# One block sum of a split down projection, made by VectorE instead of by DMA

## The reference, cut to what matters

```python
def rms_norm(x, g):
    xf = x.astype(jnp.float32)
    y = xf * lax.rsqrt(jnp.mean(xf * xf, axis=-1, keepdims=True) + RMS_EPS)
    return (y * g.astype(jnp.float32)).astype(x.dtype)

def swiglu(h, w_gate, w_up, w_down):
    return (jax.nn.silu(h @ w_gate) * (h @ w_up)) @ w_down

h = rms_norm(x, g_ffn1_pre[l])
x = x + 0.5 * rms_norm(swiglu(h, w_ffn1_gate[l], w_ffn1_up[l], w_ffn1_down[l]), g_ffn1_post[l])
...                                   # stick-breaking attention and retention, merged, projected, added to x
h = rms_norm(x, g_ffn2_pre[l])
x = x + 0.5 * rms_norm(swiglu(h, w_ffn2_gate[l], w_ffn2_up[l], w_ffn2_down[l]), g_ffn2_post[l])
```

## Time and profile before

| | value |
| --- | --- |
| median of three runs | 1460.89 us |
| profiled execution, its own time | 1462.79 us |
| its span, first to last instruction | 1460.9 us |
| busy in the span | PE 95%, PEld 85%, DVE 70%, ACT 53%, POOL 9% |
| mean granted TensorE clock | 0.979 of full speed |
| first down stage, unit 0 to 55 start | 346.42 to 522.54 us |
| second down stage, unit 0 to 55 start | 1276.26 to 1449.15 us |
| plain DMAs, page part 3 | 158.35 MB on SP's and ACT's queues, 34.0% of 16 engines' span |
| accumulating DMAs, page part 3 | 33.56 MB on POOL's queue, 12.5% |

### The profile page before, as it was taken

The page is one execution under the profiler, slowest core; times in us unless marked ns, Lnnn a source line. Parts: engine busy times, 40 slices in busy tenths (PEclk is TensorE's granted clock), DMA queues, the critical chain, the costliest instruction groups (busy, mean ns, idle before and its releaser), DMA issues.

```text
span 1460.9 us, 22674 instructions
## 1 busy us (share of the span) xinstructions
PE 1385.0 (95%) x8648; PEld 1236.7 (85%) x8648; DVE 1019.0 (70%) x1084; ACT 770.1 (53%) x1029; POOL 133.4 (9%) x180
## 2 busy tenths in 40 slices
PE   6999999998798989999989999989999999959997
PEld 6999999997686878767768888789999999948876
DVE  6877788775795954656664343687777887649786
ACT  6554555444676743647763323554445544457763
POOL 0000000001322000332320000000000000023300
PEclk9999999999899999999999999999999999989999
DMA  5323333326999563221112354233233332299974
GB/s 194 102 90 97 115 115 105 97 85 203 285 218 242 178 211 100 74 58 58 44 44 83 90 155 165 86 114 102 85 102 115 115 102 94 94 314 224 254 182 130
DMA packets 161639, 194.48 MB, mean 133 GB/s; under 512 B 6064, under 2 KB 116912, under 8 KB 161456
## 3 DMA queue, kind: packets, MB, share of 16 engines
q1 hardware_dynamic: 143456, 158.35, 34.0%
q0 software_dynamic: 17408, 33.56, 12.5%
q10 hardware_dynamic: 720, 1.84, 0.4%
HBM read 187.43 MB, written 6.29 MB: 133 GB/s over the span
## 4 chain that ended last, share of the span: by engine, by line
PE 81%; DMA 8%; DVE 6%; ACT 3%; issue 1%; POOL 1%; SPq 1%; ACTq 0%; DVEq 0%; POOLq 0%
PE ps L675 14%; PE ps L677 14%; PE ps L678 14%; PE ps L641 5%; PE ps L775 5%; PE ps L777 5%; PE ps L776 5%; PE ps L643 5%; PE ps L642 5%; DMA d_sum<-w_ffn_down 4%; DMA w_raw<-w_ffn_down 3%; PE ps L950 1%; PE ps L648 1%; PE ps L650 1%; PE ps L649 1%
## 5 line engine op out<-in xcount | busy, mean ns | idle before, releaser
L675 PE MATMUL ps<-s_hi,w_hi 128*128 128x256 f32 x960 | 273.2, 285 | 4.8 <-DVE w_lo L1554 4.8
L677 PE MATMUL ps<-s_lo,w_hi 128*128 128x256 f32 x960 | 272.9, 284 | 0.0
L678 PE MATMUL ps<-s_hi,w_lo 128*128 128x256 f32 x960 | 272.9, 284 | 0.0
L675 PE MATMUL ps<-a_hi,w_hi 128*128 128x256 f32 x816 | 232.7, 285 | 3.2 <-DVE a_lo L1509 3.0
L678 PE MATMUL ps<-a_hi,w_lo 128*128 128x256 f32 x816 | 232.4, 285 | 0.0
L677 PE MATMUL ps<-a_lo,w_hi 128*128 128x256 f32 x816 | 232.4, 285 | 0.0
L1127 ACT ACTIVATE w_hi<-w_sum 128x1024 fp32r<-128x1024 f32 x120 | 123.9, 1056 | 175.5 <-DVE w_sum L1581 80.4
L775 PE MATMUL ps<-w_hi,l_hi 128*128 128x512 f32 x448 | 179.2, 400 | 37.0 <-DVE w_lo L1718 37.0
L675 PEld LDWEIGHTS ps<-s_hi,w_hi 128*128 128x128 f32 x960 | 185.6, 193 | 5.1 <-DVE w_lo L1554 5.1
L677 PEld LDWEIGHTS ps<-s_lo,w_hi 128*128 128x128 f32 x960 | 185.7, 193 | 0.0
L678 PEld LDWEIGHTS ps<-s_hi,w_lo 128*128 128x128 f32 x960 | 185.6, 193 | 0.0
(11 more groups left out here) (192 smaller groups left out, 2582.1 us busy)
## 6 DMA issues: line engine op xcount, KB each, us to landing
w_raw<-w_ffn_gate SPq DMA_DIRECT2D x64, 512.0 KB, 4.6
w_raw<-w_ffn_up SPq DMA_DIRECT2D x64, 512.0 KB, 4.9
d_sum<-w_ffn_down POOLq DMA_DIRECT2D x64, 512.0 KB, 12.8
w_raw<-w_ffn_down SPq DMA_DIRECT2D x48, 512.0 KB, 4.9
w_raw<-w_in SPq DMA_DIRECT2D x44, 512.0 KB, 3.9
d_sum<-w_ffn_down SPq DMA_DIRECT2D x32, 512.0 KB, 11.3
x_mid<-x_tok SPq DMA_DIRECT2D x8, 512.0 KB, 4.9
x_tok<-x_mid SPq DMA_DIRECT2D x8, 512.0 KB, 11.0
```

What stands on the lines that cost most here:

```text
L675: pe.matmul(o, wh, hi[:, k, :], start=first and f == 0 and k == 0, stop=False, skip_group_check=True)
L677: pe.matmul(o, wh, lo[:, k, :], start=False, stop=False, skip_group_check=True)
L678: mm = pe.matmul(o, wl, hi[:, k, :], start=False, stop=last and k == KH - 1, skip_group_check=True)
```

## The change

The order of SP's queue changes, and T1 is made in another way. SP loads `d_sum`'s units 0 to 3 with B12 once product 2 of the last pair is over, and units 4 to 7 once product 5 is; ACT negates four units each in turns 0 and 1 instead of two each in turns 0 to 3. For T1 both B12's and B11's unit q come into the raw ring (slots 0 and 1 for even q, 2 and 3 for odd q), and DVE writes their difference to `d_sum` (`sum_t1_down`), two units a turn in turns 14 to 17. Gone with it in each FFN are the eight loads of B11 into `d_sum`, eight negations and eight accumulating DMAs. The loads of `x_tok` go behind those of T1 and the gains, and the fourth round of `down_sum` from turns 12 to 15 to turns 20 to 23.

```diff
-            - (PRODUCTS - 3) * DOWN_UNITS // SLOTS * ((u >= U_V) + (u >= U_END)))
+            - (PRODUCTS - 5) * DOWN_UNITS // SLOTS * ((u >= U_V) + (u >= U_END)))
...
                 sp_eng.wait_ge(t_done, (fi + 1) * N_T)
-                for slot in (RAW11, RAW21, RAW12):
-                    fetch(slot, down_block((0, 0), slot))
+                fetch(RAW11, down_block((0, 0), RAW11))
+                fetch(RAW21, down_block((0, 0), RAW21))
+                sp_eng.wait_ge(unit_done, ud - PRODUCTS + PE_ORDER.index(2) + 1)
+                for q in range(4):
+                    sum_load((0, 1), q)
+                fetch(RAW12, down_block((0, 0), RAW12))
                 fetch(RAW22, down_block((0, 0), RAW22), (w_lo_done, ud))
-
-                sp_eng.wait_ge(unit_done, ud)
-                for q in range(DOWN_UNITS):
+                sp_eng.wait_ge(unit_done, ud - PRODUCTS + PE_ORDER.index(5) + 1)
+                for q in range(4, DOWN_UNITS):
                     sum_load((0, 1), q)
                 for q in range(SLOTS, DOWN_UNITS):
                     fetch(q % SLOTS, down_block((0, 0), q), (w_lo_done, ud + q - SLOTS + 1))
 
-                if fi:
-                    sp_eng.wait_ge(x_left[0], 32)
-                    sp_eng.wait_ge(x_left[1], 32)
-                for t in range(TT):
-                    sp_eng.dma_start(x_tok[:, t, :], x_src[tok(t), :]).then_inc(x_back, 16)
+                for q in range(DOWN_UNITS):
+                    used = (w_lo_done, ud + SLOTS + 2 * q + 2) if q < 2 else (t1_made, DOWN_UNITS * fi + q - 1)
+                    fetch(2 * (q % 2), down_block((0, 1), q), used)
+                    fetch(2 * (q % 2) + 1, down_block((0, 0), q))
 
                 for q in range(SLOTS):
-                    fetch(q, down_block((1, 0), q), (w_lo_done, ud + SLOTS + q + 1))
-
-                for q in range(DOWN_UNITS):
-                    sp_eng.wait_ge(w_lo_done, ud + DOWN_ORDER.index(4) * DOWN_UNITS + q + 1)
-                    sum_load((0, 0), q)
+                    fetch(q, down_block((1, 0), q), (t1_made, DOWN_UNITS * fi + 7 + q // 2))
...                                    # the gains stay here; x_tok's four loads come behind them
-                    for first, begin in ((0, 0), (8, 9), (16, 14)):
-                        if begin <= n < begin + CHUNKS:
-                            for q in (2 * (n - begin), 2 * (n - begin) + 1):
-                                negate(fi, ud, first, q)
+                    if n < 2:
+                        for q in range(4 * n, 4 * n + 4):
+                            negate(fi, ud, 0, q)
+                    if 9 <= n < 9 + CHUNKS:
+                        for q in (2 * (n - 9), 2 * (n - 9) + 1):
+                            negate(fi, ud, 8, q)
...
-                    act_eng.wait_ge(r_full[q], 64 * fi + 16 * ph)
+                    if m == 5:
+                        act_eng.wait_ge(t1_made, DOWN_UNITS * fi + q + 1)
+                    else:
+                        act_eng.wait_ge(r_full[q], 48 * fi + 16 * ph)
...
-                    if n < 4 * CHUNKS:
+                    if n < 3 * CHUNKS:
                         down_sum(fi, n)
+                    elif 5 * CHUNKS <= n < 6 * CHUNKS:
+                        down_sum(fi, n - 2 * CHUNKS)
+                    if 14 <= n < 14 + CHUNKS:
+                        sum_t1_down(fi, ud, 2 * (n - 14))
+                        sum_t1_down(fi, ud, 2 * (n - 14) + 1)
...
+            def sum_t1_down(fi, ud, q):
+
+                turn = raw_turn(ud) + 2 + q // 2
+                slot = 2 * (q % 2)
+                dve.wait_ge(raw_full[slot], turn * 16 + 16)
+                dve.wait_ge(raw_full[slot + 1], turn * 16 + 16)
+                dve.wait_ge(w_lo_done, ud + DOWN_ORDER.index(4) * DOWN_UNITS + q + 1)
+                dve.tensor_tensor(d_sum[:, q, :], w_raw[:, slot, :], w_raw[:, slot + 1, :], ALU.subtract
+                                  ).then_inc(t1_made, 1)
...
-                for step, (j, d) in enumerate(((1, 1), (0, 0), (1, 0), (0, 1))):
+                for step, (j, d) in enumerate(((1, 1), (0, 0), (1, 0))):
```

More of the change, by code:

```diff
@@ L355, in build @@
         r_full = [sem(f"r_full{q}") for q in range(DOWN_UNITS)]
+        t1_made = sem("t1_made")
         r_neg, d_copied, d_summed, y_half, y_whole = (
@@ L563, in ffn_loads @@
                     gain(G_POST2)
+                sp_eng.wait_ge(unit_done, ud)
+                if fi:
+                    sp_eng.wait_ge(x_left[0], 32)
+                    sp_eng.wait_ge(x_left[1], 32)
+                for t in range(TT):
+                    sp_eng.dma_start(x_tok[:, t, :], x_src[tok(t), :]).then_inc(x_back, 16)
                 u = ud + DOWN_ORDER.index(2) * DOWN_UNITS
@@ L1255, in unit_hi @@
                 if m in (1, 2, 3):
-                    turn = raw_turn(ud) + {1: 0, 2: 2, 3: 4}[m] + q // SLOTS
+                    turn = raw_turn(ud) + {1: 0, 2: 6, 3: 8}[m] + q // SLOTS
                     act_eng.wait_ge(raw_full[q % SLOTS], turn * 16 + 16)
@@ L1267, in negate @@
                 else:
-                    act_eng.wait_ge(r_load[q], 32 * fi + (16 if first == 0 else 32))
+                    act_eng.wait_ge(r_load[q], 16 * fi + 16)
                 act_eng.activation(d_sum[:, q, :], d_sum[:, q, :], ACT.Copy, scale=-1.0).then_inc(r_neg, 1)
@@ L1982, in weight_sums @@
                         else:
-                            pool.wait_ge(r_neg, 24 * fi + DOWN_UNITS * (0, 0, 1, 2)[step] + q + 1)
+                            pool.wait_ge(r_neg, 16 * fi + DOWN_UNITS * (0, 0, 1)[step] + q + 1)
                         src = wd.rearrange("(g j p) c -> p g j c", j=2, p=P)[:, 2 * q:2 * q + 2, j, d * T:(d + 1) * T]
```

## The result

The changed kernel takes 1437.44 us (median; 1435.48 to 1439.06) against 1460.84 in the same comparison: 23.4 us less, a ratio of 0.9843 with a 95% interval of 0.9821 to 0.9865. The profiled execution took 1436.81 and spans 1434.7. The forecast was 1429.2: right in sign and 8.2 short. The time lies inside the outer range of 1419 to 1443, but 0.4 above the main band (1422 to 1437, given 0.62), in the one that was given 0.18, "ring dearer or start weaker".

What follows compares the result with a forecast made beforehand. PE, busy in 95% of the span, bounds the kernel, so only its gaps count. Gains of 14.9 + 14.2 + 2.3 + 1.6 - 1.3 = 31.7 us off 1460.9 gave 1429.2; range 1422 to 1437 (0.62), outer 1419 to 1443.

Steps and rivals of the forecast that it cites:

- ring dearer or start weaker: Band for slower ring loads in T1's phase or a smaller gain at the stage start: 1437 to 1458 us, chance 0.18.
- The pace: Down stages: PE takes 2.72 us a unit without a gap, so a turn is 5.44.
- the early loads: Start of each down stage, units 0 to 8: loads issued earlier gain 14.9 and 14.2 us.
- T3: Units from 8 on: last of eight accumulating DMAs lands by 387.3, 2 us of slack before unit 15, no stall.
- Start, the term left out: Units 0 to 8: 4.5 us lost a stage, 2.8 before unit 2 and 1.7 in units 2 to 8.
- T1, the step that failed: Units 32 to 40, T1 from the ring: 3.0 us lost a stage against 5.3 and 4.6, gaining 2.3 and 1.6.
- the ring is dearer: Rival: T1's pairs land later, 1439 us total at a landing of 7, 1453 at 9; shares chance 0.18.
- Unit 48: First down stage only: the moved `down_sum` fills DVE and makes unit 48 late, 1.3 us lost.
- Everything is hidden: Rival: pairs land within 3.8 us, T1 costs nothing and unit 48 is in time; 1422 us, chance 0.12 for below.
- the start gives little: Rival: T3 or unit 4 late again, a stall of up to 10 us a stage, 1449 us; shares chance 0.18.
- Slower than before: Rival: T1's ring loads land after 12.7 us, 23 lost plus some 5 by half clocks a stage; 1479 us, chance 0.05.
- Step 3: Moved work: 1.3 us lost at unit 48 of the first stage; later `x_tok` loads cost nothing.

Runs made afterwards that it cites:

- experiment 4: Changed kernel with two negations a turn in turns 0 to 3 instead of four in turns 0 and 1, loads still early: 1433.6 us, ratio 0.9823.
- experiment 10: Experiment 9 with the negations a turn later, two each in turns 1 to 4 instead of 0 to 3: 1424.2 us, ratio 0.9762.
- Experiments 5: Changed kernel, but only 64 of 1024 columns of B11's block are loaded for T1: 1424.1 us in one run.
- experiment 6: Changed kernel with whole loads, but each T1 subtraction on DVE covers only 64 of 1024 columns: 1427.6 us in one run.
- experiment 9: Experiment 8 with T1's sums in turns 13 (two), 15 (two), 16, 17 (one each) and 18 (two): 1424.8 us, ratio 0.9763.
- experiment 1: Kernel before with only the early loads and four negations a turn; T1 stays with negation and accumulating DMA: 1441.2 us, ratio 0.9875.
- experiment 8: Experiment 7 plus two negations a turn in turns 0 to 3 and the fourth round of `down_sum` in turns 18 to 21: 1433.6 us, ratio 0.9827.
- experiment 7: Changed kernel with T1's sums spread, two in turn 12, then one in each of turns 13 to 18: 1437.5 us, ratio 0.9846.
- experiment 3: Changed kernel with T1's sums a turn earlier, in turns 13 to 16 instead of 14 to 17: 1433.9 us, ratio 0.9827.

## Why the prediction was right in sign and 8 us short

- **The pace, the early loads, T3.** Right. Unit 8 was forecast for 372.7 and starts at 373.67. Unit 2 lost 2.9 (2.8 forecast), with ACT's order as the cause: experiment 4 took the gap to 0.80 by moving negations alone. T3's last accumulating DMA lands at 384.13 (the bound was 387.3), and nothing is lost from unit 9 to 31.
- **Start, the term left out.** The sum had 4.5 a stage, 5.6 and 5.9 came. The 1.7 a stage taken for units 2 to 8 came only as 1.1 at unit 4, since the clock did not fall after the first gap in either stage; the last part below shows that this was luck. The walk stopped at unit 4. ACT's timeline has the rest, at units 6 and 7:

```profile
363.45 1.07 ACT L1274 ACTIVATE w_hi<-w_raw 128x1024 fp32r<-128x1024 f32 x1 [1.73 <-DMA w_raw<-w_ffn_down]
367.80 1.06 ACT L1274 ACTIVATE w_hi<-w_raw 128x1024 fp32r<-128x1024 f32 x1 [3.28 <-DMA w_raw<-w_ffn_down]
```

  These loads share the DMAs with T3's accumulating ones: they were issued at 354.67 and 355.81 and landed after 8.7 and 11.6. The 4.1 for one of each kind was in the working for T3, but not used for the ring beside it. Units 7 to 9 came 1.4 and 1.7 late, and the start as a whole fell 2.4 short over both stages. In experiment 10, where fewer accumulating DMAs run by then, the start loses 0.7 and 1.7.
- **T1, the step that failed.** Forecast 3.0 a stage, measured 7.3 and 5.6: 7.0 of the 9.4 by which the down stages fell short. Two terms of the walk failed, about equally.
  - *The landing of a pair behind another.* The walk had a load land 4.0 after issue and the next 1.35 later. With the walk's zero at unit 26's start, 422.75, sum 2 came as walked. Pair 3 took 8.1 from its first issue to its last landing against 6.9 walked: in the window of the first refill 323 GB/s moved, not 393, and bytes of pair 4 were already among them. Sum 3 ended at 437.0 against 435.6, sum 5 was 1.3 late, sum 7 2.6 and unit 36's low part 2.6 late. The median landing, 4.6, was the forecast one; but a round ends with its last load, and the last took up to 7.7. Without the clock, T1 lost 5.6 and 3.9 for the 3.0 forecast.
  - *The clock behind the gap, put at nothing.* Unit 36 ran at a mean granted clock of 0.61 and 0.68, partly at 1.2 GHz and partly at 2.4. It took 459.90 - 455.49 - 2.72 = 1.7 too long in the first stage, and units 36 and 37 together 1.8 in the second. The sum held none of it, though the earlier trace rows show such a spell after the gaps of the start. Over both stages this is 3.5 of the 7.0.

  This is the rival "the ring is dearer", in its mild form. One of the prediction's own signs of being wrong, loads of the ring that take over 7 us to land, was met by a single load (7.7). Experiments 5 and 6 show the loop of refill and sums as the cause of the gap, and experiment 9 removes the loss whole.
- The Trainium skill's page "DMA: Bandwidth & Descriptors", section "Anatomy of one DMA", has 2.0 us plus the bytes at 436 GB/s, by which 3.2 for one load is an estimate; the page fits this to GpSimd's path. Here SP's loads landed after 3.6 at least and 7.7 at most, so the rule, by which the prediction would have had T1 nearly free, did not hold, least of all with two pairs in flight.
- **What T1 was compared with.** The gain was booked against before's 5.3 and 4.6. For the whole change that is the right base, but not for what T1's new way is worth: that price did not outlive the early loads, and experiment 1 has 9.1 and 7.8. The two parts are not additive (alone -19 and +3, together -23 by medians).
- **Unit 48.** Forecast 1.3 in the first stage only; measured 1.3 and none. That the moved `down_sum` is the cause is borne out in part: where it is not moved (experiment 1) nothing is lost there, and where it stands two turns earlier (experiment 8) 0.6.
- **Rivals.** "Everything is hidden" and "the start gives little" did not happen. "Slower than before" was refuted for this order, but its mechanism is real (experiment 7).

- **x_tok.** Step 3 put its loads at nothing, and in the changed kernel that holds. It does not with T1's loss gone (experiment 9).

Open: what a different place for the loads of x_tok and the gains in SP's queue would win in experiments 9 and 10, since the trace shows them ahead of unit 44's load but no run moved them. What makes units 46 and 48 late there (1.0 and 1.9 in experiment 9) was not followed up; unit 48's own load had landed at 474.18, 10.8 before it starts.

## What to carry to other kernels

When a producer on an in-order engine waits for a small ring, price the loop (last landing of the refill plus the work that frees it) against the consumer's turn; if it is longer, a head start moves the stall and takes away only a part of it (experiment 3). Spacing the uses removed it here, once the refill no longer met the other queue's DMAs (experiment 9 against 7). Price the last landing with all loads in flight, not the median, and the slower clock behind a gap with the gap. And after a gain upstream, price the old way anew before crediting what replaces it: the DMAs that were nearly in time no longer are.

## What the runs showed of the hardware

- **One gap, two outcomes of the clock.** The gap before unit 2 is 2.69 or 2.70 at twelve stage starts, two in each of six kernels (the changed one, experiments 1, 3, 5, 6 and 7). At nine of them unit 2 takes 2.8, at three 4.4, 4.4 and 5.3. In the changed kernel the first matmul after it takes 0.47 and unit 3 starts 2.81 later (above). In experiment 5 PE did the same work up to there and waited as long, and the clock fell (units 2 and 3):

```profile
354.83 0.76 PE L783 MATMUL ps<-w_hi,l_hi 128*128 128x512 f32 x1 [2.70 <-DVE w_lo L1736]
...
360.09 0.63 PE L783 MATMUL ps<-w_hi,l_hi 128*128 128x512 f32 x1
```

  Unit 2 took 5.26 instead of 2.72, so two executions may differ by 2.5 us at such a place.
- **A plain load beside accumulating ones waits for their bytes.** In experiment 7 four such loads took 8.0 to 12.7 us to landing, 11.8 in the median, against a median of 4.6 for the same loads in a stretch without them. Most of it is the bytes in flight: from 420.5 to 431.1 the queues moved 2.08 MB of plain and 0.76 MB of accumulating DMAs, which at the 393 and 206 GB/s of the earlier trace rows is an estimate of 9.0 us for these 10.6.
- **What a pair of loads takes depends on what is in flight.** In the changed kernel two loads of 512 KB took 4.9 to 5.1 us from the first issue to the last landing where at most one other load was still in flight at their issue, and 7.2 and 8.1 where another pair had been issued 1.9 and 1.1 us before.
